# Mixture-of-experts kernel: which of the 128 slots of an expert's block a token's rank is given

## The reference, cut to what matters

```
g_sel  = argmax(hf @ w_rg + b_rg)                    # one group of 4
top_v, top_i = top_k(e_in, 2)                        # two experts of the 8 in it
dest   = pstarts[e_sorted] + (arange(a) - starts[e_sorted])   # rank of the token in its expert
rows   = zeros(...).at[dest].set(h[tok_sorted])      # blocks of 128 rows, one expert each
y      = (silu(xb @ w1[e]) * (xb @ w3[e])) @ w2[e]
out    = zeros((t, d)).at[tok_sorted].add(y[dest] * w_sorted)
```

## Time and profile before

| | us |
|---|---|
| median of 3 runs | 1617.85 |
| lowest and highest | 1616.94, 1618.38 |
| span of the profiled execution | 1615.0 |
| TensorE (PE) busy in it | 1557.4 (96%) |
| VectorE busy | 1257.8 (78%) |
| ScalarE busy | 804.4 (50%) |
| GpSimd busy | 353.5 (22%) |
| time of the SP queue's packets, share of 16 DMA engines | 55.9% |
| granted TensorE clock, mean | 0.990 |

### The profile page before, as it was taken

One profiled execution on the slowest core, in us unless ns is written; L12 is line 12 of the kernel. 1 busy time (PEld: TensorE's weight loads), 2 busy tenths in 40 slices (PEclk: granted clock), 3 DMA queues, 4 the chain that ended last, 5 costly groups with the idle time before them and its releaser, 6 DMA issues.

```text
span 1615.0 us, 23288 instructions
## 1 busy us (share of the span) xinstructions
PE 1557.4 (96%) x9097; PEld 1334.4 (83%) x9097; DVE 1257.8 (78%) x1698; ACT 804.4 (50%) x878; POOL 353.5 (22%) x273
## 2 busy tenths in 40 slices
PE   5999999999999999999999998999999999999993
PEld 3777788878889999999999977888888888887771
DVE  4668877755838898887555568999999999898985
ACT  4222232334333223313243356887887878777773
POOL 2310000000000000002000202366655544333221
PEclk9999999999999999999999999999999999999997
DMA  9965223424434332234222657999999999999966
GB/s 339 319 201 181 80 86 91 138 79 148 130 91 144 118 88 77 78 88 143 75 79 84 216 197 296 389 392 385 383 366 379 381 381 384 377 373 368 371 246 237
DMA packets 219025, 362.48 MB, mean 224 GB/s; under 512 B 19807, under 2 KB 168383, under 8 KB 193562
## 3 DMA queue, kind: packets, MB, share of 16 engines
q1 hardware_dynamic: 196476, 323.10, 55.9%
q0 software_dynamic: 21792, 35.72, 7.6%
q10 hardware_dynamic: 646, 2.15, 0.3%
HBM read 363.16 MB, written 32.34 MB: 245 GB/s over the span
## 4 chain that ended last, share of the span: by engine, by line
PE 76%; DMA 11%; DVE 8%; issue 2%; DVEq 1%; ACT 1%; SPq 1%; POOLq 0%; POOL 0%; ACTq 0%
PE z L2933 16%; PE z L2935 16%; PE z L2934 16%; DMA wr<-in_w_dram 8%; PE z L910 5%; PE z L908 5%; PE z L909 5%; DVE wl L1287 3%; PE z L925 3%; PE z L926 2%; PE z L927 2%; PE q L2824 2%; DMA ada<-in_w_ada_dram 1%; DVE conv L2353 1%; PE q L899 1%
## 5 line engine op out<-in xcount | busy, mean ns | idle before, releaser
L1287 DVE TENSOR_TENSOR wl<-wr,whr 128x2048 fp32r<-128x2048 f32 x196 | 442.4, 2285 | 0.8 <-ACT whr L1099 0.5
L1099 ACT ACTIVATE whr<-wr 128x2048 fp32r<-128x2048 f32 x196 | 373.2, 1915 | 87.3 <-DMA wr<-in_w_dram 60.2
L2933 PE MATMUL z<-h_hi,w_hi 128*128 128x272 f32 (+1 forms) x1248 | 406.7, 326 | 2.3 <-DVE h_lo L2172 1.8
L2935 PE MATMUL z<-h_hi,w_lo 128*128 128x272 f32 (+1 forms) x1248 | 402.5, 323 | 0.0
L2934 PE MATMUL z<-h_lo,w_hi 128*128 128x272 f32 (+1 forms) x1248 | 401.3, 322 | 0.0
L2172 DVE TENSOR_TENSOR w_lo<-w_raw,w_hi 128x1024 fp32r<-128x1024 f32 (+1 forms) x168 | 179.5, 1069 | 127.5 <-ACT w_hi L1871 127.5
L2933 PEld LDWEIGHTS z<-h_hi,w_hi 128*128 128x128 f32 x1248 | 234.7, 188 | 28.3 <-issue 7.3
L2935 PEld LDWEIGHTS z<-h_hi,w_lo 128*128 128x128 f32 x1248 | 234.4, 188 | 16.6
L2934 PEld LDWEIGHTS z<-h_lo,w_hi 128*128 128x128 f32 x1248 | 234.8, 188 | 15.7 <-issue 0.2
L908 PE MATMUL z<-whr,xTh 128*128 128x512 f32 x528 | 208.8, 396 | 0.0
L910 PE MATMUL z<-wl,xTh 128*128 128x512 f32 x528 | 206.1, 390 | 0.0
(11 more groups left out here) (482 smaller groups left out, 2297.4 us busy)
## 6 DMA issues: line engine op xcount, KB each, us to landing
wr<-in_w_dram SPq DMA_DIRECT2D x198, 1024.0 KB, 20.8
w_raw<-in_w_in_dram SPq DMA_DIRECT2D x104, 512.0 KB, 3.8
ada<-in_w_ada_dram SPq DMA_DIRECT2D x6, 2048.0 KB, 14.2
w_raw<-in_w_branch_dram SPq DMA_DIRECT2D x48, 256.0 KB, 2.8
w_raw<-in_w_out_dram SPq DMA_DIRECT2D x16, 512.0 KB, 4.1
ada_h<-in_w_ada_dram SPq DMA_DIRECT2D x2, 2048.0 KB, 15.3
ada_u<-in_w_ada_dram SPq DMA_DIRECT2D x2, 2048.0 KB, 9.7
ada_m<-in_w_ada_dram SPq DMA_DIRECT2D x2, 2048.0 KB, 10.9
```

The lines of the kernel that those rows point to most:

```text
L1099: act.activation(whr[n % HN][:], wr[n % RN][:], ACT.Copy).then_inc(m_hi, 1)
L1287: return dve.tensor_tensor(out, a, b, op)
L2933: pe.matmul(out, w_hi[w][:, k, :], hi[:, k, t0:t1], start=(k == 0), stop=False)
L2935: last = pe.matmul(out, w_lo[w][:, k, :], hi[:, k, t0:t1], start=False, stop=(k == kn - 1))
```

## The change

`io128` no longer holds 0 to 127 in order. It is written by four instructions of 32 columns each. Column 32 j + 4 a + b (j and b from 0 to 3, a from 0 to 7) holds the rank 8 (j // 2) + 64 (j % 2) + a + 16 b. So the partitions fall into 16 groups of eight, {4 a .. 4 a + 3} and the same 32 further on, in the lower and in the upper half of the partitions, and group m holds the ranks m, m + 16, ... m + 112.

```diff
@@ -1762,8 +1762,10 @@
             pool.drain()
-            pool.iota(io128[:], pattern=[[1, P]], base=0, channel_multiplier=0,
-                      allow_small_or_imprecise_dtypes=True).then_inc(rt_const, 1)
+            for j in range(4):
+                i128 = pool.iota(io128[:, 32 * j:32 * j + 32], pattern=[[1, 8], [16, 4]], base=8 * (j // 2) + 64 * (j % 2),
+                                 channel_multiplier=0, allow_small_or_imprecise_dtypes=True)
+            i128.then_inc(rt_const, 1)
             pool.drain()
```

## The result

The changed kernel takes 1603.74 us (median, 1603.45 to 1603.84), the kernel before beside it 1617.96. The ratio is 0.9914, with a 95% interval from 0.9899 to 0.9928: 14.2 us less, where 9.2 were forecast. In a later run (`again`) it was 1603.71 against 1617.24, 13.5 us less.

What follows compares the result with a forecast made beforehand. The fullest DMA engines were taken to pace late expert blocks, TensorE the others. Savings of 8.75 us (loop) and 0.4 (end), 9.2 in all, took the 1615.0 span to 1605.8; plus 2.85 gave 1608.6 us, range 1605.8 to 1613.

Steps and rivals of the forecast that it cites:

- growth of 0.81 us per block: Weight chunks in the expert blocks: landing time rises 0.81 us per block, so the last-landing resource needs 18.56 us.
- Step 3: Expert blocks: even rows cut the fullest engine's load from 18.56 towards 17.57 us per block, saving 8.75 us.
- thin margin of 0.18 us: Expert blocks: DMA's reserve per block with even rows, 17.57 us of load under PE's 17.75.
- 2.42 us per MB: SP's weight queue: engine time per MB, making a block's six chunks 15.25 us per engine.
- One sign: Gathers and scatters: bigger blocks land no later, fitting engines tied to eight fixed partitions, or a fixed cost.
- Steps 1 and 2: Table setup and compute: four `io128` instructions are covered by a wait; other engines' work and row counts unchanged; 0 us.
- step 4: After the blocks: an evenly dealt base gather lands earlier, cutting DVE's wait; 0.4 us, between 0 and 1.99.
- The 2.85 us between span and median: Whole kernel: offset added to the forecast span of 1605.8 us to get the time.
- the stretch ahead of T(3): Block ahead of T(3), taking 18.64 us: 0.89 us possible gain, left out of the sum, counted in the range.
- DMA as a whole as the bound: Late blocks: all engines truly full, so time stays at 1617.9 or gains 1 to 2 us; chance 0.10.
- No tie between slots and engines: Indirect DMAs: rows go to engines in order of valid rows, already even, so time stays 1617.9; chance 0.04.
- The slower case: Expert blocks: memory limits, and accumulating rows on all 16 engines worsen it; 20 us more, 1638; chance 0.04.

Runs made afterwards that it cites:

- again: The changed kernel measured once more beside the kernel before: 1603.71 us against 1617.24, ratio 0.9914.
- mirror: Kernel before with ranks filled from partition 127 downwards, crowding the other half: 1617.42 us, ratio 0.9997.
- eight: Changed kernel with ranks 0 to 63 dealt evenly over the lower 64 partitions, 64 to 127 over the upper: 1609.82 us, ratio 0.9952.
- adjacent: Kernel before with ranks dealt over sixteen groups of eight adjacent partitions: 1611.07 us, ratio 0.9963.
- no_scatter: Kernel before, old slot order, with every result row but token 0's left out of the scatters: 1604.37 us, ratio 0.9919.
- thin_late: Kernel before, old slot order, with scatters of blocks 20 to 29 writing at most token 0: 1605.60 us, ratio 0.9928.
- copies_before: Kernel before with a second, plain scatter of result blocks 0 to 29 to an unread DRAM tensor: 1655.56 us, ratio 1.0239.
- copies_after: Changed kernel with a second, plain scatter of result blocks 0 to 29 to an unread DRAM tensor: 1605.50 us, 1.8 us more than the change.

## Why the prediction was right and wrong

**Right: the bound and the resource.** The step from the growth of 0.81 us per block to 18.56 us for the fullest engine, and from there to 18.52 us in late blocks, holds: moving rows between engines, with nothing else changed, moves both the landing times and the blocks (`mirror`, `eight`, `adjacent`). The parts of the chunks, which the prediction didn't have, show the same: half of them land in 6.4 us and the rest up to 20 us later. Step 3, the loop, was forecast at 8.75 us and measured 7.47 + 1.03 = 8.50. The load of 17.57 us with even rows was named as a thin margin of 0.18 us. It was wider: with 0.16 us x 4 to 5 rows more on each engine, 18.2 us by that count, chunks still landed in a steady 10.5 us. So 2.42 us per MB, 15.25 us a block, was too high a rate for the weights; their packets at 309 ns make 14.8 us. One sign was weaker than it looked: that small and large blocks scatter in the same time. A fixed time, the other reading that the prediction named, covers most of it (9.8 us almost without rows in `no_scatter`). Steps 1 and 2 stand: the four table instructions took 0.64 us together at the same place.

**Wrong: step 4, the end**, forecast at 0.4 us with 1.99 as its bound, measured 3.5. I bounded it by DVE's wait for the base gather, as if only the last gather mattered and all of DVE's work ahead of it stayed where it was. The wait alone gave 1.8 us, nearly its whole bound, of which 0.5 were lost again behind it; the other 2.2 us came from `gs`, which the step didn't have at all. What I left out is that the queue of the earlier trace rows doesn't vanish with the last chunk. The last chunks took 26 us to land where they now take 7, and everything issued behind the loop (`fgb`, the scatter of block 30, through it the tile loads, and by DVE's order in the end `gs`) stood in that queue. The landing time of `fgb`, 24.3 us, was in the profile of before and I didn't ask for it. `thin_late` shows this cause apart from the even deal.

**Wrong: the base of the sum.** The 2.85 us between span and median joined one quick execution to the median of others. With the 1.8 us that the runs show (1.7 to 1.9), my own sum would have given 1607.6. That is 1.0 us of the miss.

**Left at nothing: the stretch ahead of T(3)**, 0.89 us in the range, 1.07 measured in the first pair. It isn't settled. T(3) stands at 1024.8 and 1025.4 us in two profiles of the change, at 1025.9 in the one of before, at 1025.6 to 1026.0 in `thin_late`, `no_scatter`, `mirror` and `eight`, in `adjacent` and `copies_before` at 1025.3, `copies_after` at 1025.1. About half of it looks like the change's.

Together: 3.1 (end) + 1.1 (ahead of T(3)) + 1.0 (base) - 0.3 (loop) = 4.9 us, the distance from 1608.6 to 1603.7.

**The rivals.** DMA as a whole as the bound, given 0.10, is refuted by `copies_after`. No tie between slots and engines, 0.04, is refuted by the change itself, by `eight` and by `adjacent`: without a tie all three would take the time of before. The slower case, memory that gets worse when all 16 engines accumulate, has no trace: the rate rose. The figure of about 358 GB/s as a core's share (the Trainium skill, HBM Reference, Specifications (TRN2), the effective rate per core) was no limit here; with one core running the program the loop moved 402.

## What to carry to other kernels

A DMA is done when its fullest engine is, so count rows for the fullest engine and not the mean: a block that is part empty should be empty evenly over the groups of partitions {4a to 4a + 3, and 32 further}, which cost nothing here but another table of constants. Read the time from issue to landing along a loop: if it grows while the pacing engine holds its pace, as here, some DMA engine is behind, and what it lacks at the end of the loop delays everything that is issued next, so a fix is worth the loop's excess and the backlog too. Take the offset between span and time from pairs of the same run.

## What the runs showed of the hardware that was not expected

- The mean busy share of the 16 DMA engines over ten late blocks was 1.00 at 374 GB/s, 1.01 at 388 and, with a second scatter, 1.02 at 402. The share doesn't tell an even load from one in which half of the parts of each chunk land up to 20 us after the others.
- One row of 4 KB more on the fullest engine cost 0.16 us of the loop (plain scatter, 1.29 us for 8), and its packet took 159 ns. A row of the accumulating scatter took 327 ns, twice as long.
- Indirect scatters in late blocks landed in 11.5 us (median) before, 10.7 with the change and 9.8 with no row but token 0's written: their landing time tells little of their rows.
